# Sample differential attention moved from the last stage into the prompt's indexed attention

## The reference, cut to what matters

```python
def _diff_attend(q, kv, q_pos, lam):
    ...
        s = jnp.einsum('btghmd,bsgmd->btghms', qg, k) * scale
        p = _masked_softmax(s, mask)
        attn = p[..., 0, :] - lam * p[..., 1, :]
        o = jnp.einsum('btghs,bsgd->btghd', attn.astype(v.dtype), v)
...
def _dsa_attend(q, qi, wi, kv, kidx, q_pos):
    ...
        score = jnp.einsum('bth,bths->bts', wib * (IDX_HEADS ** -0.5), jax.nn.relu(idx_s))
        top_s, top_i = lax.top_k(score, n_sel)
        ...
        p = _masked_softmax(s, ok[:, :, None, None, :])
...
    y = jnp.concatenate([o_c * jax.nn.silu(z_c), o_d * jax.nn.silu(z_d)], axis=-1) @ w_out
    return x + gate * y, (diff_kv_new, dsa_kv_new, kidx_new)
```

## Time and profile before

| | us |
|---|---|
| median of 3 runs | 2084.7 |
| lowest, highest | 2082.84, 2085.32 |
| the profiled execution | 2079.67 |
| its span in the profile | 2077.9 |

### The profile page before, as it was taken

One profiled execution on the slowest core, in us unless ns is written; L12 is line 12 of the kernel. 1 busy time (PEld: TensorE's weight loads), 2 busy tenths in 40 slices (PEclk: granted clock), 3 DMA queues, 4 the chain that ended last, 5 costly groups with the idle time before them and its releaser, 6 DMA issues. The chain is left out here.

```text
span 2077.9 us, 27607 instructions
## 1 busy us (share of the span) xinstructions
PE 1692.5 (81%) x10319; PEld 1026.2 (49%) x10319; DVE 1066.2 (51%) x2625; ACT 510.1 (25%) x1098; POOL 264.1 (13%) x358
## 2 busy tenths in 40 slices
PE   3599999956999987975999899985856895486766
PEld 2477666533445433545665566653553442243443
DVE  3113772187767632233049899916764885021323
ACT  3100001066555500003111001014533651010122
POOL 0111120002544300000000000002103430000000
PEclk9799999977999997997999999997987997598878
DMA  6521450071000076611111101100002003989672
GB/s 263 221 71 55 171 194 21 2 279 52 1 1 1 1 255 166 178 57 48 52 45 40 42 33 42 42 0 0 1 1 82 1 1 92 265 208 221 193 182 65
DMA packets 85910, 189.33 MB, mean 91 GB/s; under 512 B 11558, under 2 KB 48524, under 8 KB 78289
## 3 DMA queue, kind: packets, MB, share of 16 engines
q1 hardware_dynamic: 58032, 120.13, 18.8%
q0 software_dynamic: 10464, 46.45, 6.3%
q10 hardware_dynamic: 17280, 20.98, 4.2%
HBM read 172.57 MB, written 19.12 MB: 92 GB/s over the span
## 5 line engine op out<-in xcount | busy, mean ns | idle before, releaser
L846 PE MATMUL banks<-hT,w_in 128*128 128x352 f32 x1632 | 485.9, 460 | 3.9 <-ACT mix L974 3.9
L846 PEld LDWEIGHTS banks<-hT,w_in 128*128 128x128 f32 x1632 | 310.7, 191 | 176.4 <-ACT mix L974 4.4
L842 PE MATMUL banks<-w_in,hT 128*128 128x264 f32 (+5 forms) x1008 | 225.7, 380 | 18.7 <-DMA w_in<-in_w_in 18.7
L2408 PE MATMUL banks<-w_out,mix 128*128 128x512 f32 x512 | 235.4, 617 | 2.4 <-DVE sel_mask L2711 1.7
L842 PEld LDWEIGHTS banks<-w_in,hT 128*128 128x128 f32 (+1 forms) x1008 | 176.5, 189 | 56.5 <-DMA w_in<-in_w_in 19.2
L2408 PEld LDWEIGHTS banks<-w_out,mix 128*128 128x128 f32 x512 | 99.1, 198 | 124.6 <-issue 120.6
L2423 DVE TENSOR_TENSOR y<-banks,gate_rows 128x512 f32<-128x512 f32 x32 | 22.1, 692 | 230.7 <-PE banks L2408 230.7
L1467 POOL TENSOR_SCALAR nsa_p<-nsa_p,nsa_sum,gates 128x640 f32<-128x640 f32 (+7 forms) x128 | 100.4, 795 | 205.0 <-DVE nsa_sum L1407 205.0
L1296 ACT ACTIVATE nsa_p<-nsa_p,nsa_negmax 128x640 f32<-128x640 f32 (+7 forms) x128 | 92.6, 725 | 29.0 <-DVE nsa_negmax L1285 28.5
L1285 DVE CUSTOM_DVE_ANT_0 nsa_p<-banks,wide_masks 128x640 f32<-128x640 f32 (+7 forms) x128 | 84.0, 703 | 25.6 <-PE banks L1271 25.6
L1957 DVE TENSOR_SCALAR_CACHE_REDUCE dsa_mask<-mix,prompt_top_tried 128x384 bf16<-128x384 f32 (+5 forms) x96 | 85.9, 943 | 1.3 <-DVE kv_rows L906 0.2
(11 more groups left out here) (522 smaller groups left out, 2347.3 us busy)
## 6 DMA issues: line engine op xcount, KB each, us to landing
w_in<-in_w_in SPq DMA_DIRECT2D x24, 1056.0 KB, 5.0
ds_ring<-in_diff_pairs SPq DMA_DIRECT2D x88, 256.0 KB, 6.7
ada_w<-in_l_ada_w SPq DMA_DIRECT2D x8, 1536.0 KB, 7.3
ns_ring<-in_sel_pairs SPq DMA_DIRECT2D x88, 128.0 KB, 2.9
ds_ring<-in_dsa_pairs SPq DMA_DIRECT2D x88, 128.0 KB, 3.4
ds_ring<-in_diff_pairs ACTq DMA_DIRECT2D x40, 256.0 KB, 10.0
ada_w<-in_l_ada_w SPq DMA_DIRECT2D x8, 1024.0 KB, 13.7
w_out<-in_l_w_out SPq DMA_DIRECT2D x4, 2048.0 KB, 16.5
```

Of the source, the lines that this page charges most:

```text
L842: last = pe.matmul(bank[0:rows, 0:n], k.hT[:, a, r0:r0 + rows], w[:, j % slots, a, 0:n], start=(a == 0), stop=(a == KT - 1))
L846: last = pe.matmul(bank[:, 0:cn], w[:, j % slots, a, m * P:(m + 1) * P], k.hT[:, a, c0:c0 + cn], start=(a == 0), stop=(a == KT - 1))
L2408: last = pe.matmul(k.bank[u % 2][0:n, :], k.mix[:, a, r0:r0 + n], self.w[:, a, h * 512:(h + 1) * 512], start=a == 0, stop=a == KT - 1)
```

## The change

The 8 differential sample units leave the last stage. The last stage keeps the 4 indexed units, with the three finishing steps of the differential result ahead of them (`mix_early` is gone). The prompt's indexed attention gets a function of its own, `attend_indexed`: its units are now two heads of each half, so 16 units and 72 steps, with 4 turns and two matmuls of 256 columns a step. `indexed_order` puts sample unit u at step 2 + 8u: its keys, one step on its exponentials, three steps on its turn (bank 4), four steps on its values (bank 7), six steps on its end. The counts of the search come in two of every three steps from step 6 on; preparation and final passes of the search are spread over steps. The ring of the sample has 4 places for keys and 6 for values (3 differential chunks). SP issues all of its pages: chunks 0 and 1 in `sample_index` once 8 of 16 index tiles have been turned, the rest in the attention.

```diff
@@ dsa_prompt
-            units.append(dict(tile=i, n=n, first=0, branch=None, steps=n // P, jobs=score_jobs([*range(4)], n), v=k.v["dsa"],
+            for a in (0, 2):
+                units.append(dict(tile=i, n=n, a=a, steps=n // P, jobs=score_jobs([a, a + 1], n), mask=sel[:, starts[i]:starts[i] + n], head=heads_of(i)))
...
+        ring = SampleRing(k, st, "maps", sample, *MAP_UNITS, 2 * NS)
         with ExitStack() as ws:
-            sample_index(k, ws)
-            search = SampleSearch(k, ws, k.qiT[0:NS, :, :].rearrange("p a n -> p (a n)"))
-            attend_pairs(k, "dsa", units, 4, None, chain(keep_dsa_sample(k, k.nc.vector), search.steps(k.nc.vector)), search)
+            sample_index(k, ws, ring)
+        attend_indexed(k, units, 4, SampleMaps(k, st, ring), keep_dsa_sample(k, k.nc.vector), SampleSearch(k, st))
...
+def indexed_order(units, maps):
+    base = attend_schedule(units)
+    steps = sum(1 for e in base if e[0] == "keys")
+    period = (steps - 8) / len(maps.units)
...
+        at = int(2 + u * period)
+        for n, what in ((0, "map_keys"), (1, "map_exp"), (3, "map_turn"), (4, "map_values"), (6, "map_end")):
+            due.setdefault(at + n, []).append((what, u, 0))
+        if un["new"]:
+            due.setdefault(at + 7, []).append(("map_join", u, 0))
...
+def attend_indexed(k, units, base, M, queries, search):
...
+        looks = [g for g in range(6, len(step_at)) if g % 3 < 2][:search.COUNTS]
...
+            @block.sync
+            def _(sp):
+                for n in range(2, len(M.R.chunks)):
+                    M.R.load(sp, n)
...
+                    elif what == "map_turn":
+                        for half in range(2):
+                            pe.wait_ge(copied[half], step_at[behind] + 1)
+                        M.turn(pe, u)
+                        map_turned = u
+                    elif what == "map_values":
+                        M.values(pe, u)
+                    elif what == "keys":
+                        if map_turned is not None:
+                            M.banks_read(pe, map_turned)
+                            map_turned = None
+                        turn(u, x)
+                        if behind:
+                            values(*behind)
...
@@ diff_dsa_sample_output
-        units = [dict(blocks=4, size=2, q=k.diff_q, q_new=k.diff_q_new, width=2 * P, new_mask=k.tailb[:, :], group=g, part=x, parts=4, pairs=2,
...
-        order = mix_early(order, last_diff)
+        order = [("diff", 0), ("diff", 1), ("diff", 2)] + order
...
@@ sample_index
+            @block.sync
+            def _(sp):
+                sp.wait_ge(turned, 8)
+                for n in range(2):
+                    ring.load(sp, n)
```

More of the change, by code:

```diff
@@ L36 @@
 SAMPLE_UNITS = ((4, 9), (4, 10))
+MAP_UNITS = (4, 6)
 GROUPS = DB // GB
@@ L1297, in exponentials, with attend_pairs @@
         last.then_inc(self.exped, 1)
-def attend_pairs(k, name, units, base, blocks=None, between=None, search=None):
+def attend_pairs(k, name, units, base, blocks=None, between=None):
     nc = k.nc
@@ L1321, in attend_pairs @@
         is_blocks = lambda u, s: "blocks" in units[u] and s == units[u]["steps"] - 1
-        out_banks = 2 if search is None else 1
-        out_bank = lambda u: k.bank[6 + units[u]["tile"] % out_banks]
+        out_bank = lambda u: k.bank[6 + units[u]["tile"] % 2]
         with nc.Block() as block:
@@ L1427, in finish @@
                     dve.tensor_tensor(z, out_bank(u)[:, :].rearrange("p (a q) -> p a q", q=P), z, ALU.mult).then_inc(A.finished, 1)
-                if search:
-                    for _ in range(3):
-                        next(between)
                 due, ended = [], []
@@ L1435, in _ @@
                         sums(*due.pop(0)[1:])
-                    while ended and e - ended[0][0] >= 2 and not search:
+                    while ended and e - ended[0][0] >= 2:
                         finish(ended.pop(0)[1])
@@ new lines, in put @@
+        def put(dve, g, parts):
+            o_rows = k.map_acc
+            for x, (o, c) in enumerate(parts):
+                if x == 0:
+                    k.dve_order.link(dve, dve.tensor_scalar(o_rows[:, g, :], o, c, None, ALU.mult))
+                else:
+                    k.dve_order.link(dve, dve.scalar_tensor_tensor(o_rows[:, g, :], o, c, o_rows[:, g, :], ALU.mult, ALU.add))
+        sample = [dict(blocks=4, size=2, q=k.diff_q, q_new=k.diff_q_new, width=2 * P, new_mask=k.tailb[:, :], group=g, part=x, parts=4, pairs=2,
+                       transfers=2 * GB, load=load_pages(k, k.t["diff_pairs"]), new=x // 3,
+                       k_new=[k.diff_k_new[:, y, :] for y in range(2)], v_new=k.diff_v_new[:, :], finish=put)
+                  for g in range(GROUPS) for x in range(4)]
@@ new lines, in indexed_order @@
+def indexed_order(units, maps):
+    base = attend_schedule(units)
+    steps = sum(1 for e in base if e[0] == "keys")
+    period = (steps - 8) / len(maps.units)
+    due = {}
+    for u, un in enumerate(maps.units):
+        at = int(2 + u * period)
+        for n, what in ((0, "map_keys"), (1, "map_exp"), (3, "map_turn"), (4, "map_values"), (6, "map_end")):
+            due.setdefault(at + n, []).append((what, u, 0))
+        if un["new"]:
+            due.setdefault(at + 7, []).append(("map_join", u, 0))
+    order, g = [], 0
+    for e in base:
+        if e[0] == "keys":
+            order += due.pop(g, [])
+            g += 1
+        order.append(e)
+    for g in sorted(due):
+        order += due[g]
+    return order
@@ L1921, in steps, with read @@
-        kth = found[:, :].bitcast(F32)
-        self.count(dve, v[:, :], kth, ALU.is_gt)
+    def read(self, dve, n):
+        link = lambda ins: self.k.dve_order.link(dve, ins)
+        if n == 0:
+            link(dve.tensor_scalar(self.found[:, :], self.total, float(TOPK), -1.0, ALU.is_lt, ALU.mult))
+        elif n < self.COUNTS - 1:
+            link(dve.tensor_scalar(self.step[:, :], self.total, float(TOPK), float(1 << (31 - n)), ALU.is_ge, ALU.mult))
+        else:
+            link(dve.tensor_scalar(self.need[:, :], self.total[0:NS], -1.0, float(TOPK), ALU.mult, ALU.add))
@@ L2711, in vector @@
             dve.tensor_copy(self.selT[:, :, :].rearrange("p g n -> p (g n)"), k.bank[5][0:32, 0:GROUPS * P]).then_inc(self.read, 1)
-def mix_early(order, last_unit):
-    ends = [x for x, e in enumerate(order) if e[0] == "end" and e[1] == last_unit][0]
-    tiles = [x for x, e in enumerate(order) if e[0] == "out" and x > ends][:2]
-    out = list(order[:ends + 1]) + [("diff", 0)]
-    for x in range(ends + 1, len(order)):
-        out.append(order[x])
-        if x in tiles:
-            out.append(("diff", 1 + tiles.index(x)))
-    return out
 def nsa_sample_output(k):
@@ L2847, in key_mask @@
             return k.spreadb[:, g, :], m
[L2849 to L2856 removed]
+        units = [dict(blocks=2, size=1, q=s["q"], q_new=s["q_new"], width=P, new_mask=sel[:, PAST:PAST + NS], group=g, part=h, parts=2, pairs=4,
+                      transfers=2 * GB, load=load_pages(k, t["dsa_pairs"]), mask=key_mask, window=None, new=h,
+                      k_new=[s["dsa_k"][:, :]], v_new=s["dsa_v"][:, :], finish=finish(acc_d))
+                 for g in range(GROUPS) for h in range(2)]
         ring = SampleRing(k, st, "ds", units, *SAMPLE_UNITS[1])
```

434 lines of the change are left out of this document (380 added, 54 removed).

## The result

The changed kernel took 2102.9 us in the median of 4 runs (2102.27 to 2105.35), the kernel before 2083.8 on the same chip: a ratio of 1.0097, 95% interval 1.0079 to 1.0114. I had forecast 2048 and faster; it is slower by 1%, and outside my range of 2008 to 2078.

A forecast was written before the change was run, and what follows sets the result against it. Blocks with barriers between them, so stages sum; moving differential pages set the last stage's first 190 us, while the attention's memory system was empty. Terms -104 + 65.5 + 3 = -35.5 us gave 2048 us, range 2008 to 2078.

The forecast's parts named there:

- 1.90 per new step: Indexed attention: a two-head step takes 1.90 us, from 3.80 per old step; 2.05 taken where counts fall.
- My terms give 158: Indexed attention without sample units: the forecast's 216.5 us less 8 x 7.3 gives 158 us.
- the 216.5 I forecast: Indexed attention's whole length: head, seven periods of 24.5 us, last unit, 14 more steps and end, against 150.9 before.
- My upper bound of 2.35: Indexed attention: time per new step in us if extra copies and counts (0.25 + 0.2) fall in series.
- TensorE waits for it: Indexed attention: a search count takes about 1.5 us on VectorE with its small companions, and TensorE waits for it.
- VectorE ... stays under it: Indexed attention: sample units add 20 us to VectorE, which has 129 + 27 us of work and stays under the stage's length.
- The sample unit, 4.8 + 2.5 = 7.3 us: Indexed attention, per sample unit every 8 steps: 4.8 us of TensorE work plus 2.5 us of waits at the turn.
- The page floor: Indexed attention: fetching a unit's second chunk through the ring sets a period of at least 24.9 to 28.2 us.
- My rival C: Indexed attention: waits for the second chunk's pages stretch the period to 33 us, +60, total 2108; chance 0.05.
- My sign for it, key matmuls of 1.9 us: Indexed attention's changed profile: page waits over 4 us and key matmuls of 1.9 us would mean slower page-limited cases.
- Last stage, -104: Last stage without differential units: 58 to first product + 146 products and units + 23.6 tail = 228 us against 331.4.
- Indexing, +3: Sample indexing: 16 page transfers queued beside the remaining key gathers cost 3 us, between nothing and about 8.

The follow-up runs named there:

- run 7: Changed kernel without sample units and without the search's totals, reciprocal two entries behind: 184.1 us from the attention's first maximum to the last stage's first gates product.
- run 8: Kernel before, without the search's totals (product, wait and reading), counts kept: 134.5 us from the attention's first maximum to the last stage's first gates product.
- run 2: Changed kernel without sample units, final search passes no longer between the last steps: 208.0 us from the attention's first maximum to the last stage's first gates product.
- run 1: Changed kernel with only VectorE's reciprocal taken four entries behind its score job instead of two: 2083.9 us, ratio 0.997 to the kernel before.
- run 12: Changed kernel, totals at every second step; reciprocal four, three, or two entries behind (the last not counting sample entries): ratios 0.9953, 0.9946, 0.9933; further variants 0.9956, 0.9972.
- the fastest version: Changed kernel with totals at every second step and the reciprocal two entries behind, sample entries not counted: 2072.9 us, ratio 0.9933 to the kernel before.
- run 4: Changed kernel with no page transfers in the attention, all sample units using the two chunks loaded before it: ratio 1.0063 to the kernel before.
- run 9: Changed kernel without sample units, VectorE's half-turn in two banks: 218.1 us (reciprocal late), 180.3 us (no totals, reciprocal two behind), first attention maximum to last-stage gates.

## Why the prediction was wrong, by its own steps

**The step that failed: "1.90 per new step", raised to 2.05.** I had the attention's time per step by halving that of a four-head step, since transposes and scores stay the same. Without sample units 72 steps took 208.0 us, or 196 without the passes that stand bare at the end there: 2.7 each, where the old ones took 4.0 (145.0 / 36) and half of that is 2.0. My terms give 158 for the whole; the steps took 196, and 201 with what the passes cost in the changed kernel. That is 38 to 43 of the 60 us by which the stretch exceeds the 216.5 I forecast. An old step was in part a chain of hand-offs (turn, copy, count, total, maxima) that a step of two heads goes through in full. My upper bound of 2.35 put only the extra copies and counts in series, not the waits. Its terms, 0.25 and 0.2, don't follow from the rows either: by them the copies add 0.08 us a new step (0.42 less half of 0.683) and the counts 0.32. What I missed, measured:
- The bare split, 37.6 us: 25.0 busy, 12.6 idle (runs 7 and 8, without the 12 us of passes at the end). I had TensorE's transposes and scores the same and the value products at half the width; the same transposes alone were busy 15.3 us longer.
- The totals, 23.9 instead of 10.5 (runs 2, 7, 8). I wrote "TensorE waits for it" and priced VectorE's 1.5 us only. 9.1 us are their new place inside the turn, which the diff shows (the totals product ahead of the second half's transposes) and my text doesn't mention.
- Together 37.6 + 13.4 = 51.0, and with the 12 us of passes the 63.0 that run 2 shows.

**"VectorE ... stays under it"** was true of its sum, 158 busy of 277, and beside the point. Work that fits in the sum still has to be there in its turn. The two-entry delay of the reciprocal is the plainest case: sample entries stand in the same list, so the delay became shorter in time and VectorE waited 30.3 us. A later reciprocal alone is worth 19.2 us of the stretch (run 1), and with the sparser totals 22.7 to 27.6, by the rule (run 12). My text doesn't mention that line at all.

**The sample unit, 4.8 + 2.5 = 7.3 us**, took 9.5 to 10.1 (76 to 81 us for eight), the second term that failed: 18 to 23 of the 60 us. From run 2 to the changed kernel TensorE's busy time grows by 51.4 us, 6.4 a unit against 4.8, since I took the work at the high clock: keys average 2.80 us (22.4 us for eight) against 2.03, values 2.44 (19.5) against 1.93. The waits at the turn were about right, 14.7 us or 1.8 a unit against 2.5. But TensorE also waits 12.3 us, 1.5 a unit, ahead of the units' keys, most of it until VectorE has taken the maxima out of the score banks that the keys are to fill, and I had no term for that:

```profile
L1924 PE MATMUL banks<-maps_ring,diff_q 64*32 64x128 f32 x1024 | 22.4, 331 | 7.6 <-DVE dsa_negmax L2201 5.2 <-DMA maps_ring<-in_diff_pairs 1.9 <-issue 0.5
```

**The page floor** of 24.9 to 28.2 us did not bind. Map keys are 32.3 us apart on average (1622.7 to 1848.6 in seven periods), engine hand-offs set that, and the pages were there. In the fastest version waits for pages are 4.9 us, still small. My rival C has the right sign, and its 2108 us and period of 33 lie close to the 2102.9 and 32.3 measured, but by luck, since its cause is wrong: waits for pages were 1.9 us, and taking the transfers out gained 1.3 (run 4). My sign for it, key matmuls of 1.9 us, came too, behind waits for other engines. My list of rivals had none in which the engines wait for each other.

The Trainium skill ("DMA: Bandwidth & Descriptors", Issuing engines are not separate DMA queues) says that queues of different engines share the same 16 DMA engines; my floor for one issuing queue came from the rows. No run here tests the page's statement, since the case isn't limited there. The same skill's "TensorE: Matmul & The Clock Gate" (HAM oscillation) describes low clock behind waits for transfers. Here the clock of the stretch was 0.83 with 1.9 us of such waits, and 0.81 without the transfers (run 4): the idle times were waits for other engines. The sum of idle time alone doesn't give the level: the bare steps of run 9 had 50.1 us of it and a clock of 0.93, those of run 7 46.4 us and 0.89.

**Last stage, -104:** measured -118.6. Start to first product 54.5 (58), products and units 136.5 (146), tail 21.6 (23.6). Right in mechanism, 15 us too careful: most of it among the products, where keys, turns and values of the units took less than I gave them and the waits were 5.5 us instead of 9.

**Indexing, +3:** the gathers and turns took 33.0 us from the first gather to the last turn against 27.6 (1604.1 less 1571.1, and 1588.4 less 1560.8), so the page transfers beside them cost 5.4, within my bounds. The first maximum comes no later all the same (41.0 against 40.9), since the search's preparation of some 6 us had moved into the steps. (My 216.5 and 150.9 count from the start of the block, so the kernel before has these 6 us in the 150.9; in the changed kernel the first maximum comes less than 1 us into the block.)

The sum: +51 + 81 - 118.6 + 0.1 = +13.4 us (131.9 for the first two), and 10.3 ahead of the touched stages in this profile; 23.7 is the difference of the two spans.

## What to carry to other kernels

The time of a step in a pipelined loop is not the sum of its widths. Before you halve a step, take the chain of hand-offs through it, instruction by instruction on each in-order engine, and ask what covers each when TensorE's part is half as long; price the halved step between half and all of the old one: here it took 0.64 of it without totals (2.39 against 3.74 us) and 0.68 with them (2.72 against 4.03), without the passes at the end. A delay that is written as a count of list entries changes meaning when entries of another kind enter the list. And work moved into a stage that hides it by the sums can cost more than the waits it gets rid of: here 118.6 us were saved and 131.9 paid, and two lines about the order (the totals at every second step, and a later reciprocal) turned that into a gain of 0.5 to 0.7%. Last, when you take a part out of a kernel to find its price, read the end of the trace too: here the edit moved 12 us of other work to where nothing covered it, and a plain difference of two stretches charged them to the steps.

## What I had not expected of the hardware

- The granted clock of the stretch fell from 0.95 to 0.83 with 1.9 us of waits for memory, while TensorE had many waits of 1 to 4 us for other engines; with no page transfers at all it was 0.81 (run 4). The sample unit's 128 key matmuls took up to 3.64 us there instead of 2.03.
- The fixed part of an instruction shows when widths are halved. VectorE's copy out of a bank takes 683 ns for 512 columns and 423 for 256. The Trainium skill ("VectorE: DVE Perf Modes", The TRN2 errata: SBUF-src ops pay a fixed extra latency per instruction) gives such a copy 120 cycles and one per column at 0.96 GHz, from which I estimate 658 and 392 ns; the trace nearly agrees in the step (260 ns for 256 columns, 267 by the page) and has 25 to 31 ns more in all. A group of four records of TensorE's value matmuls takes 1.08 us for 512 columns and 0.65 for 256 at the high clock, so two groups of half the width are busy 1.30.
- 29 MB of transfers beside the attention cost the compute engines nothing that one execution shows (1.3 us in 277, less than the scatter).
